# Seven FFNs of 256 tokens computed as seven block products instead of eight

## The chip, the cores and the metric

One core of one Trainium2 chip runs the whole program. The metric is the device time of one execution in microseconds (us); three executions of the kernel before gave 3455.6, 3461.4 and 3465.4 us, median 3461.4.

## The reference, cut to what matters

Two small networks run one after the other on a sequence of 256 tokens of width 1024, all in fp32. Eight feed-forward parts (FFNs) take most of the arithmetic:

```python
def swiglu(y, w_gu, w_down):
    gate, up = jnp.split(y @ w_gu, 2, axis=-1)        # w_gu: 1024 x 5632
    return (jax.nn.silu(gate) * up) @ w_down          # w_down: 2816 x 1024

def half_ffn(h, m, off, g, w_gu, w_down):
    y = modulate(h, g, m[off], m[off + 1])
    return h + 0.5 * m[off + 2] * swiglu(y, w_gu, w_down)
```

The first FFN handles the 256 tokens and 256 context tokens together (512 columns); the other seven handle 256 tokens. Between them lie the mixers (rwkv, conv, gla, mla) and the norms. The modulation vectors `m` are products of a vector with large matrices, `silu(c) @ ada_w`.

## The kernel before, in words

Channels lie on the 128 partitions and tokens along the free axis, so activations are tiles of 128 x 256. `F[0]` is the FFN with 512 columns; `F[1]` to `F[7]` are the seven with 256, and only these are touched. The change reaches all engines.

**One FFN before.** SyncE loads the weights into two buffers `W` in turn (`load_gu`, L2114; `load_down`, L2121); a buffer is freed when the last matmul of the unit two before it has run (`free`, which waits on `s_mm`). A gate unit `u` (11 of them, `PAIRS`) covers 256 gate and the matching 256 up columns: two blocks of 128 (`q`), each with 8 matmuls for gate and 8 for up (L2221). ScalarE takes the Silu of gate (L2302), VectorE multiplies by up (L2427) into `H` in `ARENA`. A down unit (4 of them) gives two blocks of 128 output channels with 22 matmuls each (L2241); VectorE adds them, scaled, onto `X` (L2438). A matmul in fp32 shows in the profile as two records of MATMUL on PE and two of LDWEIGHTS on PEld, so one FFN of 256 columns has 11 x 32 x 2 = 704 records in L2221 and 4 x 44 x 2 = 352 in L2241. The loops over units are real loops of two units.

**Modulation rows.** `ada(g)` on VectorE (L2360 on, with L2370 and L2372) handles a group of four tiles of 128 x 1024: per tile one scalar_tensor_tensor of ADAW with the broadcast vector CB, summed into one column of MOD. GpSimd issues the load of a group (L2180) into one of two buffers and first waits on `s_acc` until the group two before it is through. The lists `groups` say how many groups a unit handles: `F[1]` has `[1,1,0,1,1,0,1,1,0,1,1]` for its gate units and one in each down unit, `F[2]` to `F[4]` have `few = [1,0,1,1,0,1,0,1,1,0,1]` and one in each down unit, `F[5]` to `F[7]` none. On GpSimd these loads are the only work outside the rwkv mixer.

**Between FFNs.** After the last down unit the squares (ScalarE), their sum over channels (PE with `ones`), the root (ScalarE) and `rms` or `layer_norm` (VectorE) make the next input `Y` in four pieces, on which the first matmuls of the next gate unit wait one after the other (`s_y`).

The order of work on every engine is the program's order; nothing is planned at run time.

Of the kernel before, what the change touches and what calls it, by code (L numbers as in the profile page):

```python
# [7 lines left out]
ALU = mybir.AluOpType  # L8
# [145 lines left out]
def build(nc, t, out, table_at, stop=None):  # L154

    stop = STOP if stop is None else stop
    with ExitStack() as ctx:
# [74 lines left out]
        count = {"w": 0, "t": PRE, "silu": 0}  # L232

        def ffn(gu, down, T, groups, mod, k, scale):
# [9 lines left out]
            count["silu"] += FT  # L244
            plan.append(sec)
# [1490 lines left out]
        def mla_phases(layer):  # L1736
# [166 lines left out]
            def dve(dve, V, link):  # L1903
# [84 lines left out]
        F += [ffn(f2[0], d2[0], S, [1, 1, 0, 1, 1, 0, 1, 1, 0, 1, 1] + [1] * 4, 0, 8, 0.5),  # L1988
              ffn(f1[1], d1[1], S, few, 1, 2, 0.5)]
        mixers["conv"] = conv_plan()  # L1990
        F += [ffn(f2[1], d2[1], S, few, 1, 8, 0.5),
              ffn(fi[0, 0], fo[0, 0], S, few, 2, 2, 0.5)]
        mixers["gla"] = gla_plan()
        F += [ffn(fi[0, 1], fo[0, 1], S, [0] * 15, 2, 8, 0.5),
              ffn(fi[1, 0], fo[1, 0], S, [0] * 15, 3, 2, 0.5)]
        mixers["mla"] = mla_plan()
        F += [ffn(fi[1, 1], fo[1, 1], S, [0] * 15, 3, 8, 0.5)]
# [28 lines left out]
        def x_waits(k=DT, n_x=None):  # L2026

            n_x = n["x"] if n_x is None else n_x
            return ([(s_ev, done_t[0] - (DT - k))] if done_t[0] > PRE else [(s_x, 16)]) + ([(s_xr, n_x)] if n_x else [])

        done_t = [PRE]

        def norm(layer, k, T):
            n_rs = sum_squares(T, 1.0 / D, "rms")
            add("rms", layer, 3 * k, T, n_rs, vec("norm_g", 24 * layer + 8 * k, 8), bump("y"))

        def feed(i, layer, k, w):
# [62 lines left out]
        def _(sp):  # L2100
# [65 lines left out]
        def _(pool):  # L2166
            for g, (layer, tile) in enumerate(ADA_GROUPS):
# [430 lines left out]
```

## Time and profile before

| | value |
|---|---|
| executions | 3455.6, 3461.4, 3465.4 us (median 3461.4) |
| profiled execution | 3461.62 us, its span 3459.8 us, mean granted clock 0.954 |
| PE busy | 3168.7 us (92%), 21256 records |
| weight loads busy | 2538.3 us (73%) |
| VectorE / ScalarE / GpSimd busy | 1082.5 / 454.2 / 196.6 us |
| HBM read | 509.44 MB, 148 GB/s over the span |
| largest group | L2221, 5632 matmul records, busy 1383.2 us |

PE is matmul, PEld weight load, DVE VectorE, ACT ScalarE, POOL GpSimd, SPq SyncE's DMA queue. The busy time of PE counts records that overlap in the pipeline only once, so the distance between the starts of two records, not the length of one, is the pace. "Idle before" is the wait of an engine ahead of an instruction, with what ended it. The granted clock has two levels, 1.00 (2.4 GHz) and 0.50 (1.2 GHz).

### The profile page before, as it was taken

Reading aid. Unit: us, or ns where it says so; the run is one execution under the profiler, and the core shown is the slowest. Engines: PE = TensorE matmul, PEld = TensorE weight load, DVE = VectorE, ACT = ScalarE, POOL = GpSimd, SP = SyncE. Lnnn points to the kernel's source line nnn. Section 1 sums busy time; section 2 is a strip of 40 time slices with the busy share of each in tenths; the row PEclk is TensorE's granted clock in tenths of the full one; section 3 lists DMA queues with packets and bytes.
Section 4 is the critical chain, followed back from the end, with each engine's and each line's share of the span. In section 5 each row is a group of like instructions: output and inputs, shape, how many; then the busy total and the mean of one; then the engine's idle time right before and its main releaser. Section 6 shows DMA issues by size and latency. Waiting matters only on the chain.

```text
span 3459.8 us, 48396 instructions
## 1 busy us (share of the span) xinstructions
PE 3168.7 (92%) x21256; PEld 2538.3 (73%) x21256; DVE 1082.5 (31%) x2071; ACT 454.2 (13%) x1034; POOL 196.6 (6%) x314
## 2 busy tenths in 40 slices
PE   7999998777878999999999999989799999979998
PEld 6444445676777888887888878868678878857887
DVE  1554324444355323322632332234320020023101
ACT  1000002333242100001200000023000000021000
POOL 0000001332231000000000000000000000000000
PEclk8999999898899999999999999999699999988999
DMA  5555532002102677575266756534134435412352
GB/s 221 195 174 183 198 147 70 14 4 86 62 4 88 211 250 279 204 267 209 86 202 235 265 208 240 188 102 139 55 119 148 158 105 161 148 64 73 122 164 79
DMA packets 361806, 512.84 MB, mean 148 GB/s; under 512 B 10848, under 2 KB 349856, under 8 KB 352048
## 3 DMA queue, kind: packets, MB, share of 16 engines
q1 hardware_dynamic: 350992, 364.11, 32.6%
q0 software_dynamic: 10080, 143.66, 10.6%
q8 instruction: 125, 2.05, 0.2%
q10 hardware_dynamic: 576, 2.75, 0.2%
q14 instruction: 33, 0.27, 0.0%
HBM read 509.44 MB, written 1.05 MB: 148 GB/s over the span
## 4 chain that ended last, share of the span: by engine, by line
PE 88%; DVE 5%; ACT 2%; issue 2%; DMA 2%; POOL 1%; SPq 0%; DVEq 0%; ACTq 0%; POOLq 0%
PE PS L2221 39%; PE PS L2241 20%; PE PS L488 8%; PE PS L508 4%; PE PS L657 4%; PE PS L2252 2%; PE PS L2200 2%; PE PS L1231 1%; PE PS L1325 1%; PE PS L1450 1%; PE PS L524 1%; PE PS L2274 1%; ACT ADAW L790 1%; DVE X L2532 1%; POOL W L1019 0%
## 5 line engine op out<-in xcount | busy, mean ns | idle before, releaser
L2221 PE MATMUL PS<-Y,W 128*128 128x256 f32 (+1 forms) x5632 | 1383.2, 409 | 41.3 <-DVE Y L2500 26.6
L2221 PEld LDWEIGHTS PS<-Y,W 128*128 128x128 f32 x5632 | 1075.7, 191 | 348.0 <-issue 207.5
L2241 PE MATMUL PS<-ARENA,W 128*128 128x256 f32 (+1 forms) x2816 | 688.4, 407 | 13.5 <-DVE ARENA L2427 7.3
L2241 PEld LDWEIGHTS PS<-ARENA,W 128*128 128x128 f32 x2816 | 536.7, 191 | 165.1 <-issue 90.7
L2427 DVE TENSOR_TENSOR ARENA<-SIL,PS 128x256 f32<-128x256 f32 (+1 forms) x176 | 79.9, 454 | 1011.8 <-ACT SIL L2302 857.7
L2372 DVE SCALAR_TENSOR_TENSOR ADAW<-ADAW,CB 128x1024 f32<-128x1024 f32 x272 | 319.3, 1219 | 6.1 <-DMA ADAW<-in_ada_rows 5.9
L2302 ACT ACTIVATE SIL<-PS 128x256 f32<-128x256 f32 (+1 forms) x176 | 72.3, 411 | 1355.1 <-PE PS L2221 1355.1
L488 PE MATMUL PS<-Y,W 128*128 128x256 f32 (+2 forms) x816 | 183.4, 388 | 32.1 <-DVE Y L2500 22.2
L2438 DVE SCALAR_TENSOR_TENSOR X<-PS,HG,X 128x256 f32<-128x256 f32 x72 | 34.1, 482 | 544.0 <-PE PS L2241 544.0
L488 PEld LDWEIGHTS PS<-Y,W 128*128 128x128 f32 (+2 forms) x816 | 156.4, 192 | 58.9 <-DVE Y L2500 23.0
L508 PE MATMUL PS<-W 64*64 64x64 f32 x4608 | 117.8, 227 | 45.9 <-ACT W L754 24.5
L657 PE MATMUL PS<-Y,W 128*128 128x256 f32 x560 | 134.6, 402 | 24.4 <-DVE Y L2464 15.3
L2314 ACT ACTIVATE Y<-X 128x512 f32<-128x512 f32 x60 | 36.0, 627 | 884.6 <-DVE X L2517 437.7
L657 PEld LDWEIGHTS PS<-Y,W 128*128 128x128 f32 x560 | 111.8, 202 | 47.6 <-DVE Y L2464 16.2
L508 PEld LDWEIGHTS PS<-W 64*64 64x64 f32 x4608 | 104.6, 139 | 57.0 <-issue 27.8
L2180 POOL DMA_DIRECT2D ADAW<-in_ada_rows x68 | 36.1, 531 | 1534.2 <-DVE ADAW L2372 1454.3
L488 PE MATMUL PS<-ARENA,W 128*128 128x256 f32 x480 | 106.9, 383 | 14.4 <-issue 13.8
L488 PEld LDWEIGHTS PS<-ARENA,W 128*128 128x128 f32 x480 | 92.0, 192 | 27.9 <-issue 14.6
L2252 PE MATMUL PS<-Y,CT 128*128 128x256 f32 (+1 forms) x208 | 63.9, 468 | 12.8 <-ACT Y L2314 12.8
L2370 DVE SCALAR_TENSOR_TENSOR JUNK<-ADAW,CB 128x1024 f32<-128x1024 f32 x56 | 68.2, 1217 | 3.0 <-DMA ADAW<-in_ada_rows 3.0
L2200 PE MATMUL PS<-SC,ARENA 128*128 128x2 f32 x256 | 52.3, 343 | 18.1 <-DMA CT<-in_table 18.1
L2252 PEld LDWEIGHTS PS<-Y,CT 128*128 128x128 f32 x208 | 44.8, 218 | 30.2 <-issue 23.9
(346 smaller groups left out, 2160.8 us busy)
## 6 DMA issues: line engine op xcount, KB each, us to landing
ADAW<-in_ada_rows POOLq DMA_DIRECT2D x68, 2048.0 KB, 8.3
W<-in_ffn_w_gu SPq DMA_DIRECT2D x88, 1024.0 KB, 7.5
W<-in_ffn_in SPq DMA_DIRECT2D x88, 1024.0 KB, 6.7
W<-in_ffn_w_down SPq DMA_DIRECT2D x32, 1408.0 KB, 9.0
W<-in_ffn_out SPq DMA_DIRECT2D x32, 1408.0 KB, 8.7
W<-in_even_w_in SPq DMA_DIRECT2D x40, 512.0 KB, 4.6
W<-in_e_w_in SPq DMA_DIRECT2D x34, 512.0 KB, 4.9
ARENA<-in_ada_columns SPq DMA_DIRECT2D x4, 2048.0 KB, 25.3
```

The lines of the kernel that those rows point to most:

```text
L488: last = mm(PS[idx % 4][0:m_, 0:S], wide(c, kt, n_)[:, k, q * P:q * P + m_], x(k), start=(k == 0), stop=(k == kt - 1))
L508: last = mm(to, x, y, start=(k == 0), stop=(k == len(pairs) - 1))
L657: last_ = mm(PS[at[f] % 4][:, 0:S], wide(c, DT, cols)[:, k, q * P:(q + 1) * P], Y[:, k, off:off + S], start=(k == 0), stop=(k == DT - 1))
L2180: pool.dma_start(ADAW[:, g % 2].rearrange("p a b -> p (a b)"), t["ada_rows"][g * P:(g + 1) * P, :])\
L2200: last = mm(PS[c][:, 2 * q:2 * q + 2], PREW[:, c, k, q * P:(q + 1) * P], SC[:, :, k], start=(k == 0), stop=(k == DT - 1))
L2221: last = mm(o, gate_up(c)[:, g, k, q * P:(q + 1) * P], Y[:, k, 0:T], start=(k == 0), stop=(k == DT - 1))
L2241: last = mm(PS[idx % 4][:, 0:T], wide(c, FT)[:, k, q * P:(q + 1) * P], H[:, k, 0:T], start=(k == 0), stop=(k == FT - 1))
L2252: last = mm(NORM_PS[:, 0:T], ones, src[:, k, 0:T], start=(k == 0), stop=(k == kt - 1))
L2302: A(SIL[:, u % 2, 0:T], PS[bank % 4][:, 0:T], ACT.Silu).then_inc(s_silu, 1)
L2370: V.scalar_tensor_tensor(JUNK[:, :], w, 1.0, CB[:, 1], ALU.mult, ALU.mult, accum_out=MOD[:, 4, tile + i:tile + i + 1]).then_inc(s_junk, 1)
L2372: ins = V.scalar_tensor_tensor(w, w, 1.0, CB[:, 1 if layer > 1 else 0], ALU.mult, ALU.mult, accum_out=MOD[:, layer, tile + i:tile + i + 1])
L2427: V.tensor_tensor(H[:, f, 0:T], SIL[:, q, 0:T], up, ALU.mult).then_inc(s_ev, per // 2)
```

## The change: seven block products in place of eight

For `F[1]` to `F[7]` the product of weights and tokens is cut into 2 x 2 blocks, and the blocks of the result are formed from seven block products (Strassen's scheme in Winograd's form) in place of eight. Tokens are cut into two halves of `HT` = 128 columns, and the contraction into two halves. In a gate unit the two weight rows of blocks are gate and up; in a down unit they are the two blocks of 128 output channels.

The names in the new code: `A11`..`A22` are weight blocks and `B11`..`B22` token blocks; the weight sums are S1 = A21 + A22, S2 = S1 - A11, S3 = A11 - A21, S4 = A12 - S2, the token sums T1 = B12 - B11, T2 = B22 - T1, T3 = B22 - B12, T4 = B21 - T2. Product 1 is A11 B11, 2 is A12 B21, 3 is S4 B22, 4 is A22 T4, 5 is S1 T1, 6 is S2 T2, 7 is S3 T3. Each product of a gate unit is two blocks of 128 columns of weights x 4 steps of contraction = 8 matmuls of 128 x 128 weights on 128 tokens (16 records); each product of a down unit has 11 (22 records).

What each engine does now (the diff shows the tables, then GpSimd, PE and VectorE in this order):

- **PE** (`small_ffn`) runs the products in the order 1, 4, 2, 6, 7, 5, 3 (in the first unit 1, 2, 6, 4, 7, 5, 3), each behind its own waits. 2 is accumulated onto 1, and 5 onto 6. The units are unrolled.
- **GpSimd** makes S1 and S3 of each unit once the weights have landed (elements per partition: 1024 in a gate unit, 1408 in a down unit), then the token sums T1 to T4 of the hidden block of the unit before (128 elements each), and last issues the loads of modulation rows, each with its old wait on `s_acc`. S3 is written over A21.
- **VectorE** makes S2 and S4 of each unit at the head of the unit's work, joins the blocks out of PSUM, multiplies, and keeps the groups of modulation rows, now in three parts (two tiles, one, one) between the joins. S2 of an FFN's first unit is made before the norm's reciprocal (`first_sum`).
- **ScalarE** copies product 1 out of PSUM, takes the Silu of one half out of PSUM and of the other out of SBUF.
- **SyncE** loads the same weights as before, under the same rule for free buffers, unrolled.

```diff
+        BX, BY, BQ, BZ, BW = (0, 1), (2, 3), (4, 4), (6, 6), (7, 7)
+        FIRST_ORDER = (1, 2, 6, 4, 7, 5, 3)
+        ORDER = (1, 4, 2, 6, 7, 5, 3)
+        PRODUCT = {1: ("A11", "B11", BX), 2: ("A12", "B21", BX), 3: ("S4", "B22", BW), 4: ("A22", "T4", BQ),
+                   5: ("S1", "T1", BY), 6: ("S2", "T2", BY), 7: ("S3", "T3", BZ)}
...
+            def weight_sums(n_, c, w):
+                pool.wait_ge(s_w[c % 2], 32 * (c // 2 + 1))
+                G.tensor_tensor(w["S1"], w["A21"], w["A22"], ALU.add).then_inc(s_s1, 1)
+                pool.wait_ge(s_s1, n_ + 1)
+                G.tensor_tensor(w["S3"], w["A11"], w["A21"], ALU.subtract).then_inc(s_s3, 1)
...
+            def small_ffn(sec):
+                g = sec["group0"]
+                for u in range(PAIRS + 4):
+                    c, n_ = sec["w0"] + u, sec["n0"] + u
+                    weight_sums(n_, c, gate_blocks(c, n_) if u < PAIRS else down_blocks(c, n_))
+                    if 0 < u < PAIRS:
+                        hidden_sums(sec, u - 1)
+                    for _ in range(sec["groups"][u]):
+                        if g + 2 < len(ADA_GROUPS):
+                            rows(g + 2)
+                        g += 1
...
+                def gate_waits(u, p):
+                    fa, fd = fa0 + 3 * u, fd0 + 5 * u
...
+                    elif p == 3:
+                        pe.wait_ge(s_s4, n0 + u + 1)
...
+                    elif p == 5:
+                        pe.wait_ge(s_fd, fd + 1)
+                    elif p == 6:
+                        pe.wait_ge(s_s2, n0 + u + 1)
...
+                    elif p == 7:
+                        pe.wait_ge(s_s3, n0 + u + 1)
...
+                for u in range(PAIRS):
+                    if u:
+                        second_sum(n_, w)
+                    else:
+                        token_sums(YB, s_ty, 4 * i)
+                    fourth_sum(n_, w)
+                    if more:
+                        ada(g, (0, 1))
+                    dve.wait_ge(s_fa, fa + 1)
+                    dve.wait_ge(s_mm, product_done(sec, u, 6))
+                    V.tensor_tensor(halves(U3), halves(C1), both_banks(BY), ALU.add).then_inc(s_fd, 1)
+                    if more:
+                        ada(g, (2,))
...
+                    V.tensor_tensor(halves(U3), halves(U3), both_banks(BZ), ALU.add).then_inc(s_fd, 1)
...
+                    link(V.tensor_tensor(halves(U3), halves(U3), both_banks(BQ), ALU.add))
+                    V.tensor_tensor(HC[:, u, :, 0:HT], halves(U3), halves(S0), ALU.mult).then_inc(s_fd, 1)
+                    dve.wait_ge(s_mm, product_done(sec, u, 5))
+                    V.tensor_tensor(halves(U4), halves(C1), both_banks(BY), ALU.add).then_inc(s_fd, 1)
...
+                    dve.wait_ge(s_mm, product_done(sec, u, 3))
+                    V.tensor_tensor(halves(C12), halves(U4), both_banks(BW), ALU.add).then_inc(s_fd, 1)
+                    link(V.tensor_tensor(halves(U4), halves(U4), both_banks(BZ), ALU.add))
+                    if more:
+                        ada(g, (3,))
+                        g += 1
+                    dve.wait_ge(s_fa, fa + 3)
+                    V.tensor_tensor(HC[:, u, :, HT:S], halves(U4), halves(C12), ALU.mult).then_inc(s_ev, 7)
+                dve.wait_ge(s_ev, td)
+                token_sums({name: v[:, PAIRS - 1] for name, v in HB.items()}, s_tl, 4 * i)
```

A down unit on VectorE has S2 and S4 (1408 elements), then eight scaled additions onto `X` and three plain ones, of 128 columns each, with the group's tiles between them. Product 4 of the first down unit waits for the token sums of the last hidden block.

## Rows read from the trace of the kernel before

**Rows 1.** The page: busy time, share of the span, instructions.
```profile
PE 3168.7 (92%) x21256; PEld 2538.3 (73%) x21256; DVE 1082.5 (31%) x2071; ACT 454.2 (13%) x1034; POOL 196.6 (6%) x314
```
**Rows 2.** The chain in order of time: start us, us, what.
```profile
1395.29 154.03 PE PS L2221 x704
1550.51 76.24 PE PS L2241 x352
1904.38 16.48 DMA W<-in_ffn_w_down
```
**Rows 3.** Stretches: length, busy (x records) PE, PEld, DVE, ACT, POOL; clock, DMA, GB/s.
```profile
1395.30:1549.30 154.00, 154.00 (x704) 134.53 (x704) 45.02 (x87) 8.07 (x21) 3.69 (x7) 0.99 0.68 235
2557.70:2712.40 154.70, 153.21 (x702) 133.25 (x700) 13.83 (x34) 8.08 (x22) 0.00 (x0) 0.99 0.44 141
```
**Rows 4.** Timeline of PE, matmuls on 128 columns: start us, us, engine, line.
```profile
3146.00 0.83 PE L1825 MATMUL PS<-ADAW 128*128 128x128 f32 x6
3146.67 0.60 PE L1833 MATMUL PS<-ADAW,ARENA 128*128 128x256 f32 x2
3147.10 0.38 PE L1834 MATMUL PS<-ADAW,ARENA 128*128 128x128 f32 x2
3147.32 0.39 PE L1812 MATMUL PS<-ARENA 128*128 128x128 f32 x2
3147.64 0.48 PE L1813 MATMUL PS<-ARENA 64*128 64x128 f32 x2
3148.06 0.49 PE L1814 MATMUL PS<-CT 128*128 128x128 f32 x2
```
**Rows 5.** VectorE by shape: busy us, mean ns of one, idle before.
```profile
L1618 DVE TENSOR_TENSOR ARENA<-ARENA,ADAW 128x1024 f32<-128x1024 f32 x1 | 1.2, 1226 | 0.0
L2427 DVE TENSOR_TENSOR ARENA<-SIL,PS 128x256 f32<-128x256 f32 x154 | 64.8, 421 | 857.7 <-ACT SIL L2302 857.7
L2456 DVE TENSOR_TENSOR Y<-X,RS 128x512 f32<-128x512 f32 x32 | 22.0, 688 | 0.6
```
**Rows 6.** Timeline of GpSimd alone in the rwkv mixer.
```profile
642.31 0.58 POOL L1019 TENSOR_TENSOR W<-ARENA,W 128x192 f32<-128x192 f32 x1
647.77 1.00 POOL L1025 TENSOR_TENSOR W<-W,CT 128x384 f32<-128x384 f32 x1
```
**Rows 7.** Timeline where VectorE and GpSimd both read two SBUF operands.
```profile
956.12 1.02 DVE L947 TENSOR_TENSOR Y<-ARENA 128x512 f32<-128x512 f32 x1
956.55 1.03 POOL L1020 TENSOR_TENSOR W<-ARENA,W 128x192 f32<-128x192 f32 x1
957.17 0.96 DVE L948 TENSOR_TENSOR Y<-Y,ARENA 128x512 f32<-128x512 f32 x1
```
**Rows 8.** Timeline from the last gate unit to the first down unit.
```profile
1310.84 0.42 DVE L2427 TENSOR_TENSOR ARENA<-SIL,PS 128x256 f32<-128x256 f32 x1 [6.49 <-ACT SIL L2302]
1311.17 1.22 DVE L2372 SCALAR_TENSOR_TENSOR ADAW<-ADAW,CB 128x1024 f32<-128x1024 f32 x1
1311.58 1.59 PEld L2241 LDWEIGHTS PS<-ARENA,W 128*128 128x128 f32 x8 [1.60 <-DVE ARENA L2427]
1312.32 1.22 DVE L2372 SCALAR_TENSOR_TENSOR ADAW<-ADAW,CB 128x1024 f32<-128x1024 f32 x1
```
**Rows 9.** Timeline of VectorE: two pieces of the norm's output.
```profile
1395.06 0.68 DVE L2456 TENSOR_TENSOR Y<-X,RS 128x512 f32<-128x512 f32 x1
1396.43 0.68 DVE L2456 TENSOR_TENSOR Y<-X,RS 128x512 f32<-128x512 f32 x1
```
**Rows 10.** Stretches, columns as in rows 3: a gap and what follows.
```profile
1310.40:1312.40 2.00, 0.81 (x4) 0.74 (x5) 1.56 (x4) 0.38 (x1) 0.00 (x0) 1.00 0.65 211
1917.80:1921.20 3.40, 0.22 (x1) 0.23 (x2) 3.00 (x6) 0.37 (x1) 0.00 (x0) 1.00 0.80 270
1921.80:1925.00 3.20, 3.20 (x9) 2.57 (x8) 1.40 (x4) 0.00 (x0) 0.53 (x1) 0.50 1.09 359
```
**Rows 11.** Loads of W, 1156 to 2200 us: time to landing.
```profile
DMA to landing us min/median/max: 3.4/6.4/16.5
```

More of the change, by code:

```diff
@@ L244, in ffn, with small_ffn @@
             count["silu"] += FT
+            plan.append(sec)
+            return sec
+        def small_ffn(gu, down, groups, mod, k, scale):
+            n_ = PAIRS + 4
+            sec = dict(kind="small", gu=gu.rearrange("(k p) n -> p k n", p=P), down=down.rearrange("(k p) n -> p k n", p=P),
+                       T=S, groups=groups, w0=count["w"], t0=count["t"], n0=count["sums"], i=count["sums"] // n_, mod=mod,
+                       k=k, scale=scale)
+            sec["fa0"] = sec["i"] * (3 * PAIRS + 4)
+            sec["fd0"] = sec["i"] * (5 * PAIRS + 6 * 4)
+            sec["td"] = sec["t0"] + 7 * PAIRS
+            sec["ends"] = [sec["t0"] + 7 * (j + 1) for j in range(n_)]
+            sec["t1"] = sec["ends"][-1]
+            count["w"] += n_
+            count["t"] = sec["t1"]
+            count["sums"] += n_
             plan.append(sec)
@@ L278, in build @@
+        s_s1, s_s2, s_s3, s_s4 = [sem(f"weight_sum{i}_ready") for i in range(1, 5)]
+        s_ty = sem("token_sums_ready")
+        s_th = sem("hidden_sums_ready")
+        s_tl = sem("last_hidden_sums_ready")
+        s_fa = sem("small_ffn_scalar_step")
+        s_fd = sem("small_ffn_vector_step")
         HP = 2 * HD
@@ L2140, in _ @@
                         load_down(sec, j, j)
+                elif sec["kind"] == "small":
+                    for j in range(PAIRS):
+                        free(sec["w0"] + j)
+                        load_gu(sec, j, j)
+                    for j in range(4):
+                        free(sec["w0"] + PAIRS + j)
+                        load_down(sec, j, j)
                 else:
@@ L2358, in _, with ada @@
             link = Chain(dve, s_dve)
[L2360 removed]
+            def ada(g, part=range(GROUP)):
                 layer, tile = ADA_GROUPS[g]
[L2363 to L2364 removed]
+                if part[0] == 0:
+                    dve.wait_ge(s_adaw[g % 2], 16 * (g // 2 + 1))
+                for i in part:
                     w = ADAW[:, g % 2, i]
@@ L2550, in _ @@
                     ffn(F[args[0]])
+                elif kind == "small":
+                    small_ffn(F[args[0]])
+                elif kind == "first_sum":
+                    first_sum(args[0])
                 elif kind == "do":
```

301 lines of the change are left out of this document (260 added, 41 removed).

## The prediction

> **What bounds the kernel now.** I read the busy times first: PE's matmuls fill 92% of the span, VectorE 31%, ScalarE 13%, GpSimd 6% [rows 1]. The chain of waits in order of time then shows an FFN of 256 tokens as two unbroken pieces of PE: 704 records in 154.03 us and 352 in 76.24 us [rows 2]. In the stretches PE is busy without a gap at a clock of 0.99, while in an FFN with modulation rows VectorE works 45.0 of 154.0 us and the DMA share is 0.68; in one without them VectorE works 13.8 us and the share is 0.44 [rows 3]. So PE's pace is the bound: 76.24 / 352 = 0.2166 us for a record of 256 columns. An FFN has 1056 such records, 228.7 us. Its small gaps are one of 1.6 us between gate and down, where PE waits for the last multiplication [rows 8], and one at the start: the input comes in pieces 1.37 us apart [rows 9], of which a piece feeds 4 records, 0.87 us, so three waits cost 1.5 us.
>
> **Fewer, but shorter matmuls.** A product of a gate unit has 16 records, seven of them 112, 11 units 1232; a product of a down unit has 22, so 7 x 22 x 4 = 616. Together 1848 records of 128 columns in place of 1056 of 256. The arithmetic falls by an eighth, but each block of weights is used for half as many columns, so the loads per unit of time nearly double. What matters is the distance between two records on 128 columns with 128 x 128 weights. In the mla mixer six run in a row and the next begins 0.67 us after the first: 0.1117 us each; two more (L1834) take 0.22 us, 0.110 each [rows 4]. I take 0.1117: 206.4 us, against 228.7. Gain 22.3 us an FFN; at 0.110 it would be 25.4. In a gate unit a product then lasts 1.79 us and the unit 12.5 us (before 13.9); in a down unit 2.46 and 17.2 us (before 19.1).
>
> On the weight loads a page speaks against this. In L1825's six records every matmul loads new weights over all 128 rows and still follows the last after 0.1117 us [rows 4], so the load runs beneath the matmul before it. The Trainium skill ("TensorE: Matmul & The Clock Gate", What overlaps and what doesn't) says that a weight load overlaps matmuls in flight only where the row group differs. By that rule load and matmul would take turns, 0.223 us a record, 413 us an FFN and some 4750 us in all; the trace does not agree.
>
> **Where each unit's sums come from.** GpSimd alone takes 0.58 us for 192 elements and 1.00 for 384 [rows 6], so 2.2 ns an element: 2.4 us for 1024, 3.2 for 1408, 0.44 for 128. VectorE takes 1.226 us for 1024 and 0.421 for 256 [rows 5]: 1.63 for 1408 and 0.29 for 128. A tile of modulation rows takes 1.22 us, and the next starts after 1.15 [rows 8], so two take 2.37. Where both engines read two SBUF operands at once, 512 elements on VectorE take 1.02 and 0.96 us [rows 7] in place of 0.688 [rows 5], and 192 on GpSimd 1.03 [rows 7] in place of 0.58 [rows 6]: factors 1.45 and 1.75.
>
> VectorE's work in a gate unit without rows is 2.45 us of sums and eight joins of 0.42, 5.8 us; with a group of rows 10.5 us. GpSimd's is 2 x 2.4 + 4 x 0.44 = 6.6 us. Both fit in 12.5 us, so the order decides, not the load.
>
> *Unit without rows behind a unit without rows.* Weights land 6.4 us (3.4 to 16.5) after their issue [rows 11], which is a whole unit ahead, so S1 and S3 exist before the unit starts or soon after. VectorE finishes the last unit 1.6 us into the new one (add 0.2 to 0.6, add, Silu, multiply) and has S2 by 3.3 and S4 by 5.0, contention counted. Product 6 starts at 5.4, product 3 at 10.7. The first join after product 6 (done 7.2) ends at 7.8, product 5 starts at 9.0. No stall; a unit with rows behind it has two tiles more (7.4) and its join ends by 7.9. Still none. ScalarE's copy of product 1 takes 0.38 us (8.07 us for 21 records of 256 columns [rows 3]) and lies under product 4.
>
> *Any unit behind a unit with rows.* GpSimd's load of the next group stands ahead of the next unit's S1, and waits until VectorE has ended the fourth tile, which now comes after product 3. With zero at the end of product 3: VectorE adds twice (to 1.07) and ends the tile at 2.35; GpSimd issues the load, 0.53 us (3.69 us for 7) [rows 3], to 3.0; S1 to 5.4; S2 under contention 1.8 us to 7.3; PE restarts 0.3 us after a release, as between multiply and down unit [rows 8]: product 6 at 7.6 in place of 5.4. S3, slowed, comes at some 9.5 and costs 0.2 more. Stall 2.4 us. If this unit has rows too, S4 ends at 9.1, two tiles under contention (3.4) at 12.5, the join at 12.9, and product 5 starts at 13.2 in place of 11.4: 1.8 more, 4.2 in all. The bounds: with no contention 1.6 and 2.0; with VectorE shut out for the whole of each GpSimd operation 4.0 and 6.3 (S2 waits for S3 and ends at 9.1).
>
> Counting the lists: `F[1]` has three units of the first and four of the second kind: 3 x 2.4 + 4 x 4.2 = 24.0 us. `F[2]` to `F[4]` have four and two: 18.0 us each. `F[5]` to `F[7]`: none.
>
> *Gate to down.* Without rows: multiply done at 1.6, three chained sums of 0.29 with links to 2.6, product 4 at 2.9 in place of 2.5: 0.4 us, against 1.6 before, a gain of 1.2. With rows: product 4 at 4.5 (2.0 late), and the join ahead of product 5 is 0.6 late: 2.6, a loss of 1.0. In the other down units the group's last tile lies ahead of the joins of product 5, so GpSimd is released 2.5 us before the unit ends, and product 6 is due 7.4 us in: no stall. The late landing in `F[3]`, 16.48 us [rows 2], stays a late landing, since it has 12.5 us in place of 13.9; its wait falls on that of product 4. Under 1 us, left out.
>
> *First unit.* Product 1 ends at 2.7, product 2 waits for ScalarE's copy (3.4) and piece four (4.1) and ends at 5.4, product 6 needs two sums of 512 elements after the last piece: 6.0. Two products are 3.6 us, so 2.4 is lost, against 1.5 before: 0.9. S2 of the first unit is made while VectorE waits for the norm's root; nothing is late by it.
>
> **The sum.** `F[5]` to `F[7]`: 22.3 - 0.9 + 1.2 = 22.6 us, three times 67.8. `F[2]` to `F[4]`: 22.3 - 0.9 - 18.0 - 1.0 = 2.4, three times 7.2. `F[1]`: 22.3 - 0.9 - 24.0 - 1.0 = -3.6. Together 71.4 us off the profiled execution's 3461.62 us (span 3459.8, with 1.8 around it): 3390 us. The median of the runs, 3461.4, is the same within 0.2.
>
> **The rivals.**
>
> *The weight load is exposed at every product.* Each of the 11 x 7 + 4 x 7 = 105 products of an FFN begins behind waits and with new blocks. Between L1812, L1813 and L1814 a pair takes 0.42 us (3147.64 to 3148.06) in place of 0.22 [rows 4]: the load was not ahead. For it: seven times as many waits as before. Against it: L1825 to L1833 and L1834 to L1812 cross a wait at 0.11 us [rows 4]; the slow pairs are those where the weights change from 128 rows to 64 and back. Price 105 x 0.20 = 21 us an FFN, 147 in all: 3537 us. It decides from 5.5 ns a record (71.4 us over 7 x 1848), that is from a mean pace of 0.117 us. Slower than before.
>
> *VectorE is shut out while GpSimd works.* Rows 7 show slowing, not shutting out, but over 0.6 us operations. Gate stalls then are 28.6 in place of 18.0 us and 37.2 in place of 24.0: 45 us more, 3435 us. The same end is reached if stalls make the clock fall: a gap of 1.6 us left it at 1.00, one of 3.4 us was followed by 0.50 for 3.2 us [rows 10], 1.6 us lost each time, and there are 25 stalls of 2.4 to 4.2 us (25 x 1.6 = 40). The Trainium skill ("SBUF — State Buffer", Who interferes with whom) has a VectorE operation with two SBUF inputs contend with GpSimd's reads, and in its Terms the loser fully blocks; that gives this rival's number, and rows 7, where both advance, agree only in part.
>
> *The stalls are small and the pace is the fast one.* With no contention 34 us less stall, with 0.110 us a record 22 us more gain: 3334 us.
>
> *No change,* by partial forms of these: for it speaks only that four of the seven FFNs gain almost nothing.
>
> **Chances.** Forecast 0.55; small stalls 0.17; shutting out or clock 0.15; exposed loads 0.10; no change 0.03. Range 3330 to 3440 us: it reaches to the second and third case and leaves out the exposed loads, no change, and the ends of these. The forecast's own range is 3360 to 3420. A change under 0.3%, 10 us, can't be told from none. Faster: 0.55 + 0.17 + 0.15 = 0.87; within: 0.03; slower: 0.10.
>
> **What would show it.** Over an FFN without rows (`F[5]`), PE should go through 1232 records in about 140 us and 616 in 69, with starts 0.11 us apart also across products. In `F[2]` the unit behind one with rows should have PE waiting 2 us for VectorE's S2 ahead of product 6, VectorE waiting for GpSimd's S1, and GpSimd for the fourth tile; the gate part of `F[1]` should last some 162 us (1232 x 0.1117 + 24.0 + 0.9). A pace above 0.117, stalls in `F[5]`, or GpSimd's 1024 elements at 3.5 us instead of 2.4 would prove me wrong.

## The result, and the profile after

The kernel with seven block products takes 3462.93 us (median of 20 runs, 3455.68 to 3467.94), the kernel before 3456.97 us (20 runs, 3449.29 to 3465.40). The ratio is 1.0017, with a 95% interval of 1.0010 to 1.0024: slower, but by less than the 0.3% named above as no change. The forecast was 3390 us, a gain of 2.1%, with a range of 3330 to 3440. The forecast was wrong, and the time fell outside the range.

The profiled execution of the new kernel has a span of 3458.8 us at a mean clock of 0.944; before it was 3459.8 us at 0.954. First its busy times (columns as in [rows 1]):

```profile
PE 3056.9 (88%) x26800; PEld 2609.0 (75%) x26800; DVE 1901.0 (55%) x3023; ACT 493.4 (14%) x1139; POOL 1052.8 (30%) x804
```

PE has less to do than before (3056.9 in place of 3168.7 us) and the span is the same: PE now stands still for 401.9 us in place of 291.1. VectorE and GpSimd have 1675 us more between them, in which their waiting for each other is counted (below). The stretches of `F[2]` (gate, down) and of `F[5]` (gate, down), columns as in [rows 3]:

```profile
1410.00:1574.00 164.00, 146.78 (x1226) 142.23 (x1227) 122.64 (x174) 13.91 (x33) 100.69 (x66) 0.97 0.60 213
1574.00:1653.00 79.00, 71.76 (x622) 71.60 (x621) 70.33 (x88) 3.20 (x8) 28.22 (x13) 0.96 0.63 220
2611.00:2753.00 142.00, 140.43 (x1231) 139.52 (x1232) 78.44 (x126) 13.90 (x33) 80.21 (x59) 0.98 0.48 155
2753.00:2827.00 74.00, 70.96 (x621) 70.80 (x620) 37.99 (x54) 1.52 (x5) 28.53 (x10) 0.98 0.46 146
```

The gate part of `F[5]` is what was forecast (about 140 us; 142). The down part has 74 us in place of the 69 forecast. `F[2]` has modulation rows: its gate part took 154 us before, now 164, and its down part 79 in place of 76. Where PE waits in the block products stands in the list of PE's waits (after the colon: total us, times, longest):

```profile
PE PS L2473 <- DVE ARENA L2716: 38.1, 7, 7.2
PE PS L2431 <- DVE ARENA L2700: 36.1, 32, 1.3
PE PS L2431 <- DVE SIL L2738: 30.3, 25, 2.2
...
PE PS L2431 <- POOL W L2281: 3.9, 25, 0.2
```

The second line is S2 ahead of product 6 (32 times, of which 25 behind a unit with rows). The third is the join after product 6, for which product 5 waits. The first, the dearest of all, is the last token sum between gate and down part: 5.4 us on average, seven times.

**The seven FFNs, one by one.** From the starts of all PE records I take each FFN apart: the distance between neighbours is 0.112 us (before 0.216), what a distance above 0.36 us (before: above 0.86) has over that is a gap, and what the others have over it is put down to PE at the lower clock. In us:

```
                               F[1]   F[2]   F[3]   F[4]   F[5]   F[6]   F[7]    sum
before: first to last matmul  231.3  231.3  235.2  234.6  233.2  233.3  233.3  1632.2
  at the pace of 0.216        228.1  in each                                  1596.7
  gaps                          1.4    1.4    3.4    3.2    2.5    2.6    3.4    17.9
  lower clock                   1.8    1.8    3.7    3.3    2.6    2.6    1.8    17.6
after: first to last matmul   250.5  243.1  242.5  243.5  215.8  217.3  215.9  1628.6
  at the pace of 0.112        207.0  in each                                  1449.0
  gaps in gate units           26.4   21.5   20.6   22.0    2.5    2.5    2.9    98.4
  gap ahead of product 4        7.4    7.4    7.4    7.4    3.2    3.2    3.2    39.2
  lower clock                   9.7    7.3    7.5    7.1    3.2    4.6    2.8    42.2
PE idle ahead of the FFN, before 4.0    4.0    4.0    8.0    4.8    4.8    4.8    34.4
PE idle ahead of the FFN, after  8.3    4.1    7.2    8.1    6.1    5.8    4.8    44.4
```

So the change gains 147.7 us of pace and gives 144 back inside the FFNs (119.7 in gaps, 24.6 by the clock) and 10 ahead of them: 6.4 us slower. The medians differ by nearly the same, 6.0. The two profiled spans don't show it: the profiled execution of before was 4.7 us above its median, the other 2.3 us below.

### The profile page after: what moved, and what is told of

Read it like the earlier page. It is cut to its first block and busy times, and to the rows that moved or that the text cites. A ratio compares the mean times of both kernels' runs of the same rounds, so it can differ in the third digit from the quotient of the medians.

```text
span 3458.8 us, 60893 instructions
## 1 busy us (share of the span) xinstructions
PE 3056.9 (88%) x26800; PEld 2609.0 (75%) x26800; DVE 1901.0 (55%) x3023; ACT 493.4 (14%) x1139; POOL 1052.8 (30%) x804
## 3 DMA queue, kind: packets, MB, share of 16 engines
q8 instruction: 207, 3.39, 0.4%
## 5 line engine op out<-in xcount | busy, mean ns | idle before, releaser
L2431 PE MATMUL PS<-Y,W 128*128 128x128 f32 x4928 | 599.1, 280 | 55.0 <-DVE Y L2866 27.5
L2431 PEld LDWEIGHTS PS<-Y,W 128*128 128x128 f32 x4928 | 578.0, 196 | 67.4 <-issue 47.0
L2279 POOL TENSOR_TENSOR ARENA<-W 128x1024 f32<-128x1024 f32 (+1 forms) x105 | 270.8, 2579 | 929.8 <-DMA W<-in_ffn_in 595.9
L2431 PE MATMUL PS<-Y,ARENA 128*128 128x128 f32 x3696 | 452.5, 280 | 66.8 <-DVE ARENA L2700 36.1
L2431 PEld LDWEIGHTS PS<-Y,ARENA 128*128 128x128 f32 x3696 | 433.5, 195 | 78.0 <-DVE ARENA L2700 42.2
L2473 PE MATMUL PS<-ARENA,W 128*128 128x128 f32 x2464 | 300.2, 283 | 38.1 <-DVE ARENA L2716 38.1
L2473 PEld LDWEIGHTS PS<-ARENA,W 128*128 128x128 f32 x2464 | 294.4, 200 | 39.2 <-issue 39.2
L2361 PE MATMUL PS<-Y,W 128*128 128x512 f32 x704 | 305.2, 597 | 2.2 <-DVE Y L2830 2.2
L2281 POOL TENSOR_TENSOR W<-W 128x1024 f32<-128x1024 f32 (+1 forms) x105 | 299.3, 2851 | 8.2
L2361 PEld LDWEIGHTS PS<-Y,W 128*128 128x128 f32 x704 | 134.8, 192 | 172.0 <-issue 171.4
L2700 DVE TENSOR_TENSOR ARENA<-ARENA,W 128x1024 f32<-128x1024 f32 (+1 forms) x105 | 167.2, 1592 | 81.3 <-POOL ARENA L2279 81.0
L2705 DVE TENSOR_TENSOR ARENA<-W,ARENA 128x1024 f32<-128x1024 f32 x77 | 151.2, 1963 | 2.4
L744 PEld LDWEIGHTS PS<-Y,W 128*128 128x128 f32 x560 | 109.7, 198 | 46.1 <-DVE Y L2830 16.2
## 6 DMA issues: line engine op xcount, KB each, us to landing
ADAW<-in_ada_rows POOLq DMA_DIRECT2D x68, 2048.0 KB, 10.4
```

The source lines that it names most:

```text
L744: last_ = mm(PS[at[f] % 4][:, 0:S], wide(c, DT, cols)[:, k, q * P:(q + 1) * P], Y[:, k, off:off + S], start=(k == 0), stop=(k == DT - 1))
L2279: G.tensor_tensor(w["S1"], w["A21"], w["A22"], ALU.add).then_inc(s_s1, 1)
L2281: G.tensor_tensor(w["S3"], w["A11"], w["A21"], ALU.subtract).then_inc(s_s3, 1)
L2361: last = mm(o, gate_up(c)[:, g, k, q * P:(q + 1) * P], Y[:, k, 0:T], start=(k == 0), stop=(k == DT - 1))
L2431: last = mm(block_bank(b, q), w[left][:, k, q * P:(q + 1) * P], YB[right][:, k], start=(k == 0 and p not in (2, 5)), stop=(k == 3), skip_g ...
L2473: last = mm(block_bank(b, 0), w[left][:, k], HB[right][:, k], start=(k == 0 and p not in (2, 5)), stop=(k == PAIRS - 1), skip_group_check= ...
```

## Why the gaps: one engine works, the other stands

The timeline behind a unit with rows in `F[2]`; product 3 of that unit ended at 1425.9, and products 1, 4 and 2 of the next last until 1431.3:

```profile
1428.05 0.42 DVE L2759 TENSOR_TENSOR ARENA<-SIL 128x256 f32<-128x256 f32 x1
1428.42 0.58 POOL L2273 DMA_DIRECT2D ADAW<-in_ada_rows  x1 [24.82 <-DVE ADAW L2628]
1429.02 2.36 POOL L2279 TENSOR_TENSOR ARENA<-W 128x1024 f32<-128x1024 f32 x1
...
1431.42 1.23 DVE L2700 TENSOR_TENSOR ARENA<-ARENA,W 128x1024 f32<-128x1024 f32 x1 [2.95 <-POOL ARENA L2279]
1431.46 3.39 POOL L2281 TENSOR_TENSOR W<-W 128x1024 f32<-128x1024 f32 x1
1432.68 3.26 DVE L2705 TENSOR_TENSOR ARENA<-W,ARENA 128x1024 f32<-128x1024 f32 x1
...
1432.70 2.05 PE L2431 MATMUL PS<-Y,ARENA 128*128 128x128 f32 x16 [1.34 <-DVE ARENA L2700]
1434.81 1.44 POOL L2288 TENSOR_TENSOR ARENA<-ARENA 128x128 f32<-128x128 f32 x1
...
1435.86 0.41 DVE L2738 TENSOR_TENSOR SIL<-JUNK,PS 128x256 f32<-128x256 f32 x1
1436.33 0.46 POOL L2290 TENSOR_TENSOR ARENA<-ARENA 128x128 f32<-128x128 f32 x1
```

The chain forecast is there step by step: the load issued behind VectorE's tile, 2.5 us after product 3, then S1 (L2279), S2 (L2700), product 6 at 6.8. But nothing is slowed by a factor. S2 needs 1.23 us, its time alone. S3 (L2281) is issued 0.04 us after it and takes 3.39: it waits 1.03 us for S2 and then takes its own 2.36. S4 (L2705) is issued 1.22 us after S3 and takes 3.26: it waits until S3 has ended, some 2.1 us, and then takes its own 1.2. GpSimd's token sum (L2288) in turn waits 1.0 for S4 and then takes its 0.46. The join L2738 reads one operand from PSUM; it takes its 0.41 whatever GpSimd does. The Trainium skill ("SBUF — State Buffer", Who interferes with whom, and Terms) says just this: a VectorE instruction with two SBUF inputs contends with a GpSimd one that reads SBUF, whoever is first holds the ports for its whole instruction, and the other fully blocks. The trace agrees to 0.1 or 0.2 us: S3 ends 2.20 us after S2, S4 1.09 us after S3 and the token sum 0.31 us after S4, each that much under its time alone.

What that does to a short operation stands between gate and down part, where product 4 waits for three chained token sums of 0.29 us:

```profile
1574.68 2.62 PE L2473 MATMUL PS<-ARENA,W 128*128 128x128 f32 x22
...
1577.34 0.29 DVE L2712 TENSOR_TENSOR ARENA<-ARENA 128x128 f32<-128x128 f32 x1
1577.67 3.52 DVE L2714 TENSOR_TENSOR ARENA<-ARENA 128x128 f32<-128x128 f32 x1
1577.86 3.16 POOL L2279 TENSOR_TENSOR ARENA<-W 128x1408 f32<-128x1408 f32 x1
1581.10 3.15 POOL L2281 TENSOR_TENSOR W<-W 128x1408 f32<-128x1408 f32 x1
1581.22 3.18 DVE L2716 TENSOR_TENSOR ARENA<-ARENA 128x128 f32<-128x128 f32 x1
...
1584.54 0.77 PE L2473 MATMUL PS<-ARENA,W 128*128 128x128 f32 x2 [7.24 <-DVE ARENA L2716]
```

S1 and S3 of the down unit run unhindered (3.16, 3.15), and the two sums on which PE waits are late by a whole one each: 3.52 and 3.18 us for 0.29 us of work. Even L2714, issued 0.19 us ahead of S1, lost. Without rows GpSimd is already through S1, and only S3 is in the way: 3.2 us.

The groups by shape (busy us, mean ns of one, idle before) show how wide this reaches. S4, and the additions onto `X`, of which the form that reads PSUM has 351 ns and the form that reads SBUF twice 1542:

```profile
L2705 DVE TENSOR_TENSOR ARENA<-W,ARENA 128x1024 f32<-128x1024 f32 x77 | 151.2, 1963 | 2.4
L2775 DVE SCALAR_TENSOR_TENSOR X<-SIL,HG,X 128x128 f32<-128x128 f32 x84 | 129.5, 1542 | 2.0
...
L2775 DVE SCALAR_TENSOR_TENSOR X<-PS,HG,X 128x128 f32<-128x128 f32 x112 | 39.3, 351 | 59.6 <-PE PS L2473 55.4 <-issue 0.5
```

**The clock.** Stretches around that gap, columns as in [rows 3]:

```profile
1581.90:1584.50 2.60, 0.00 (x0) 0.00 (x0) 2.60 (x2) 0.00 (x0) 2.35 (x1) 0.62 0.98 404
1584.60:1588.00 3.40, 3.40 (x16) 3.40 (x17) 3.37 (x3) 0.00 (x0) 0.00 (x0) 0.50 0.94 368
1588.00:1591.40 3.40, 3.40 (x27) 3.40 (x27) 2.08 (x4) 0.00 (x0) 0.00 (x0) 0.80 0.47 149
1591.40:1650.00 58.60, 58.60 (x528) 58.60 (x527) 53.34 (x68) 2.50 (x6) 20.76 (x9) 1.00 0.59 207
```

After 7.2 us without work PE runs 16 records in 3.4 us at 0.50, that is at 1.2 GHz, in place of some 30 at 2.4. A mean of 0.80 over the next 3.4 us is 1.4 us more at 0.50 and 2.0 at 1.00. The last row has the pace undisturbed: 58.60 / 528 = 0.111 us.

The small stalls look different. The first row below holds two stalls of `F[2]`'s gate part, of 1.5 and 2.3 us, and the clock stays at 1.00; the second is the one stretch at 0.50 in the middle of that part; the third is the start of the FFN:

```profile
1459.20:1468.20 9.00, 5.34 (x43) 4.77 (x42) 7.95 (x8) 0.38 (x1) 8.77 (x6) 1.00 0.91 352
1541.60:1544.80 3.20, 3.20 (x15) 3.20 (x16) 2.15 (x5) 0.00 (x0) 1.27 (x1) 0.50 0.00 0
1410.20:1415.00 4.80, 4.24 (x17) 3.65 (x18) 4.62 (x11) 0.59 (x2) 0.00 (x0) 0.50 0.25 79
```

In all seven gate parts together the clock is at 0.50 for 59 us, before for 24. Of these 42 lie at the starts of the FFNs (before all 24), and 17 in five single stretches of 3.4 us, two in `F[1]` and one each in `F[2]` to `F[4]`.

**Ahead of the norm.** S2 of an FFN's first unit stands before the norm's reciprocal:

```profile
1142.93 2.35 POOL L2281 TENSOR_TENSOR W<-W 128x1024 f32<-128x1024 f32 x1
1142.95 3.40 DVE L2700 TENSOR_TENSOR ARENA<-ARENA,W 128x1024 f32<-128x1024 f32 x1 [4.36 <-POOL ARENA L2279]
...
1146.47 1.75 DVE L2837 RECIPROCAL RS<-RS 128x256 f32<-128x256 f32 x1
```

ScalarE's root was ready at 1142.0. VectorE waited for S1 till 1142.9, S2 lost to S3 and took 3.40, and the norm, for which PE stands still, began 4.3 us late. Ahead of `F[3]` it is the same (3.2 us). Ahead of `F[5]` and `F[6]` S2 is through in time; there a piece of the norm (L2896) takes 1.97 and 1.72 us in place of 0.68, beside GpSimd's S3 of the second unit.

## The experiments

Each ratio is against the kernel before, run on the same chip, with its 95% interval; the median of before was 3457.38 us in the first four, 3451.12 in the next three, and 3452.71 in the last two. The changed kernel itself stands at 1.0017. "Gaps" are taken as in the table above.

**1. The loads of rows wait a unit.** GpSimd issues a group's load behind the next unit's S1 and S3, so these no longer wait for VectorE's fourth tile.

```diff
                     weight_sums(...)
+                    while due:
+                        rows(due.pop(0))
...
                     for _ in range(sec["groups"][u]):
                         if g + 2 < len(ADA_GROUPS):
-                            rows(g + 2)
+                            due.append(g + 2)
```

> The changed kernel, with GpSimd issuing the loads of modulation rows one unit later, behind the next unit's S1 and S3. Theory A (order and lock): the time is lost because GpSimd's load stands ahead of the next unit's S1, and because VectorE and GpSimd shut each other out when both read two SBUF operands. Then the gate gaps of the FFNs with rows, 21 to 26 us in the changed kernel, should fall to some 8 to 14 us each, the low clock should shrink with them, and the time should be 35 to 60 us below the changed kernel's, about 3410 us. Theory B (weights late): units of 12.5 us instead of 13.8 outrun the weight loads. Then nothing moves by more than 5 us.

Measured: 3404.15 us (3398.61 to 3413.73), ratio 0.9851 (0.9826 to 0.9877). The gate gaps of `F[1]` to `F[4]` fell from 90.5 to 42.9 us: that link of the chain was real. But PE's idle time ahead of `F[1]`, `F[3]` and `F[4]` rose to 11.1, 11.0 and 12.1 us. With no load in the way, the second unit's S1 and S3 now run beside the norm, and its pieces take 1.63 and 2.63 us where they took 0.69 and 0.73:

```profile
1153.21 1.63 DVE L2826 TENSOR_TENSOR Y<-X,RS 128x512 f32<-128x512 f32 x1
1154.38 2.67 POOL L2281 TENSOR_TENSOR W<-W 128x1024 f32<-128x1024 f32 x1
1154.88 2.63 DVE L2834 TENSOR_SCALAR Y<-Y,GS,MOD 128x256 f32<-128x256 f32 x2
```

The same contention, in another place, and of another kind of operation: L2834 reads one tensor from SBUF, with two factors of one element per partition. The first of its two took 2.31 us, in place of 0.41, and ended just after S3.

**2. The first down unit's weight sums behind the last token sums.**

```diff
                     c, n_ = sec["w0"] + u, sec["n0"] + u
+                    if u == PAIRS:
+                        pool.wait_ge(s_tl, 4 * sec["i"] + 4)
                     weight_sums(...)
```

> The changed kernel, with GpSimd starting the weight sums of the first down unit only after the token sums of the last hidden block. Theory A: the gap of 7.5 us ahead of product 4 in the first down unit (3.3 us in FFNs without rows) is VectorE's four small sums taking turns with GpSimd's 1408 element sums. It should shrink to 2 to 3 us (under 1 us without rows): 4 x 4.5 + 3 x 2.6 = 26 us, with clock some 30 us below the changed kernel, about 3432 us. Theory B: the gap is the weights' landing or the last multiply; it stays above 6 us and the time moves by less than 5 us.

Measured: 3428.95 us (3424.78 to 3440.66), ratio 0.9924 (0.9896 to 0.9951), 0.93% or 32 us less than the changed kernel. PE's waits for the last token sum and, new, for the join after product 6 of that unit:

```profile
PE PS L2475 <- DVE SIL L2788: 6.0, 4, 1.5
PE PS L2475 <- DVE ARENA L2718: 5.1, 7, 1.1
```

From 38.1 us to 5.1, by one wait. The down part's gaps fell by 22.9 us, and its time at the lower clock by 12.2 (from 13.4 to 1.2), while the gate part kept both. So the clock's loss there hung on this gap: each of the four gaps of 7.4 us cost some 2.0 us more than its length, each of the three of 3.2 us some 1.4.

**3. GpSimd's sums on one column.** All of GpSimd's sums shrink to one element per partition; S1, S3 and the token sums of the hidden blocks are thus left out. Everything waits for the same semaphores.

```diff
+                one = slice(0, 1)
-                G.tensor_tensor(w["S1"], w["A21"], w["A22"], ALU.add)...
+                G.tensor_tensor(w["S1"][:, 0, one], w["A21"][:, 0, one], w["A22"][:, 0, one], ALU.add)...
```

> The changed kernel with every GpSimd sum of the block products cut to one column of 128 partitions (the rest of the sums is left out), all waits and the order kept. Theory A: with no long GpSimd operation there is nothing to wait for and nobody to shut out. The FFNs should take 211 to 216 us each, gate gaps under 5 us, gap ahead of product 4 of the first down unit under 1.5 us, and the time should be about 3320 us (3305 to 3345). Theory B: gaps stay, time above 3420 us. If the low clock came from the short matmuls and not from the gaps, the FFNs would keep 10 us or more at the low clock with the gaps gone.

Measured: 3345.73 us (3340.06 to 3347.57), ratio 0.9675 (0.9655 to 0.9694): with GpSimd's work gone the change is worth 3.2%. Its S2 and S4 are back at their time alone, and the largest wait in the gate units is now a load:

```profile
L2706 DVE TENSOR_TENSOR ARENA<-W,ARENA 128x1024 f32<-128x1024 f32 x77 | 94.4, 1226 | 2.4
L2701 DVE TENSOR_TENSOR ARENA<-ARENA,W 128x1024 f32<-128x1024 f32 x77 | 94.1, 1222 | 25.2 <-POOL ARENA L2280 24.8
```

```profile
PE PS L2432 <- DMA W<-in_ffn_w_gu: 16.9, 12, 2.1
```

The idle time ahead of `F[1]` and `F[3]` is 4.0 again. I expected some 3320, and gate gaps under 5 us in each FFN; in `F[1]` to `F[4]` they are 7.4 to 10.4. The weights themselves come late, up to 2.1 us, which the stalls had covered. The low clock did not go with the gaps either: in the seven FFNs together it is at 0.50 for 64 us (103 in the changed kernel, 31 before), most of it at their starts. This run takes away both GpSimd's hold on the ports and its latency, so it doesn't tell these two apart.

**4. Block products in `F[5]` to `F[7]` alone.** `F[1]` to `F[4]` as before.

```diff
-        F += [small_ffn(f2[0], d2[0], ...), small_ffn(f1[1], d1[1], few, 1, 2, 0.5)]
+        F += [ffn(f2[0], d2[0], S, ...), ffn(f1[1], d1[1], S, few, 1, 2, 0.5)]
```

> Block products only in the last three FFNs, which have no modulation rows; the first four of 256 tokens as in the kernel before. Theory A: each of the three is 16 to 17.5 us shorter than before, less some 2 us in all for the first S2 ahead of the norms: 46 to 51 us below the kernel before, about 3409 us. A theory in which the seven FFNs are coupled (weights, queues) would give less than 35 us.

Measured: 3406.01 us (3402.66 to 3415.89), ratio 0.9861 (0.9837 to 0.9885). The three took 217.0, 215.8 and 217.8 us, against 233.3 before: the gain of 48 us is theirs, and the four with rows had cost more than that.

**5. Both orders together.** Edits 1 and 2, and in the first unit S3 behind S2 in place of behind S1.

```diff
-                pool.wait_ge(s_s1, n_ + 1)
+                pool.wait_ge(s_s2 if behind else s_s1, n_ + 1)
                 G.tensor_tensor(w["S3"], ...)
```

> The changed kernel with both earlier edits (loads of modulation rows one unit later; first down unit's sums behind the last token sums), and in an FFN's first unit GpSimd makes S3 only after VectorE's S2. Theory A (order and lock): the gains add up, save that the boundary gap of the FFNs with rows was already partly gone: 15 to 30 us below the kernel with late rows alone (3404 us), so about 3382 us (3372 to 3392); the idle time ahead of F[1] falls from 11.1 to 6 or 7 us. Theory C (VectorE's amount of work in the units with rows, not its turns with GpSimd, sets the gaps): under 10 us.

Measured: 3401.93 us (3397.59 to 3405.48), ratio 0.9854 (0.9837 to 0.9870), no better than edit 1 alone, where 3372 to 3392 was expected. The down gaps of `F[1]` to `F[4]` were 8.2 to 11.1 us, at a new place, ahead of product 5 of the first down unit:

```profile
1562.88 4.17 DVE L2634 SCALAR_TENSOR_TENSOR ADAW<-ADAW,CB 128x1024 f32<-128x1024 f32 x1
1566.98 0.08 DVE L2634 DVE_READ_ACCUMULATOR ADAW<-ADAW,CB 128x1 f32 x1
1566.98 4.15 DVE L2634 SCALAR_TENSOR_TENSOR ADAW<-ADAW,CB 128x1024 f32<-128x1024 f32 x1
```

With its load no longer waiting for VectorE, GpSimd goes from one unit's S1 and S3 to the next's with only 0.57 us between (four sums, 1553.64 to 1570.06). VectorE's S4 takes 4.46 us, the two tiles behind it 4.17 and 4.15 in place of 1.22, and the join behind those is 7.4 us late. The old place of the load had kept GpSimd out of VectorE's way here. The number alone would fit the rival, that VectorE's amount of work sets the gaps; the next two runs speak against it.

**6. The fourth tile early.** Edit 2, S3 behind S2 in the first unit, the loads where the change has them, and the fourth tile of a group beside the third, ahead of the joins after products 7, 5 and 3. In `F[2]` the fourth tile then ends 1.5 us before product 3 does, in place of 2.2 us after it.

```diff
                     if more:
-                        ada(g, (2,))
+                        ada(g, (2, 3))
+                        g += 1
...
-                    if more:
-                        ada(g, (3,))
-                        g += 1
```

> The changed kernel with the fourth tile of each group of modulation rows handled beside the third, ahead of products 7, 5 and 3, in place of the load issued later; with the edits for the first down unit and the first unit's S3. Theory A: GpSimd is released some 2 us before the unit ends in place of 2.4 us after, so S1 of the next unit is there in time, and the multiply is no longer behind a tile: gate gaps of F[1] to F[4] from 21 to 26 us down to 6 to 12, total about 3365 us (3345 to 3385), lower than with late rows. Theory C: the work of VectorE is the same, only moved, so above 3400 us.

Measured: 3361.59 us (3356.98 to 3366.78), ratio 0.9741 (0.9725 to 0.9757). Gate gaps in `F[1]` to `F[4]` 49.4 us (from 90.5), down gaps 1.2 to 2.5. VectorE's busy time, waiting counted, is 1902.3 us, as in the changed kernel (1901.0), and the kernel is 2.8% faster: what fell is not what VectorE does or waits in all, but what PE waits for it.

**7. All sums on VectorE.** GpSimd only issues loads; VectorE makes S1 to S4 at the head of a unit and T1 to T4 behind its last multiplication. The order is otherwise that of the change.

```diff
+                V.tensor_tensor(w["S1"], w["A21"], w["A22"], ALU.add).then_inc(s_s1, 1)
                 V.tensor_tensor(w["S2"], w["S1"], w["A11"], ALU.subtract).then_inc(s_s2, 1)
+                V.tensor_tensor(w["S3"], w["A11"], w["A21"], ALU.subtract).then_inc(s_s3, 1)
```

> The changed kernel with all sums on VectorE: S1 and S3 beside S2 and S4, and the token sums after each multiply; GpSimd only issues loads. VectorE's work grows by 3.7 us a gate unit, to 9.5 us without rows and 14.2 with, in a unit of 12.5 us. Theory A: no VectorE operation takes longer than it does alone. F[5] to F[7] should take 212 to 214 us (gap ahead of product 4 under 1 us), the units with rows should be bound by VectorE at some 14.5 us, 2 to 3 us of gap each, F[1] to F[4] 224 to 230 us; total 3370 to 3400 us, clearly below the changed kernel's 3462. Theory C: more work on the engine that sets the gaps makes it slower than the changed kernel, above 3465 us.

Measured: 3359.88 us (3359.51 to 3364.63), ratio 0.9736 (0.9719 to 0.9752), better than expected. Busy times:

```profile
PE 3033.9 (90%) x26800; PEld 2592.2 (77%) x26800; DVE 1954.6 (58%) x3513; ACT 492.9 (15%) x1139; POOL 196.4 (6%) x314
```

This run shows what the helper saved VectorE. VectorE executes 490 instructions more than in the changed kernel, 210 weight sums (154 of 1.22 us, 56 of 1.62) and 280 token sums of 0.29, 359 us in all, and its busy time grows by only 54. The other 305 us had thus been in its records as waiting for GpSimd, which spent 856 us to spare VectorE 54. No weight sum takes longer than alone (1217 to 1224 ns for 1024 elements). How much of the 2.8% gained is the ports' and how much GpSimd's latency the run doesn't say: S1 is also made in 1.22 us in place of 2.36, and no longer stands behind a load that waits for the fourth tile.

**8. Token sums on VectorE, weight sums on GpSimd.** Edit 6, with T1 to T4 of the hidden blocks moved to VectorE.

> As the version with the fourth tile beside the third, but the sums of a hidden pair (four of 128 columns) are made by VectorE right behind the multiplication that ends the pair, not by GpSimd. If the two engines take turns on the SBUF operands, what counts is the time that both need together: a string of four takes GpSimd some 4 to 6 us with its handovers and VectorE 4 x 0.29 = 1.2 us undisturbed. Theory (turns): the stalls ahead of product 6 and 5 in units with modulation rows shrink, 3350 to 3356 us in place of 3361.6. Rival (what stands first on VectorE decides): S2 and S4 of each unit with rows start 1.2 us later on VectorE, which is on the path, 23 units x up to 1.2 = 3375 us or more.

Measured: 3377.92 us (3373.21 to 3380.74), ratio 0.9775 (0.9760 to 0.9789): slower than edit 6. The rival was right in kind. The string stands ahead of S2, and what comes before it is late besides:

```profile
1453.11 1.13 DVE L2745 TENSOR_TENSOR ARENA<-SIL 128x256 f32<-128x256 f32 x1 [0.25 <-ACT SIL L2544]
1454.27 0.29 DVE L2700 TENSOR_TENSOR ARENA<-ARENA 128x128 f32<-128x128 f32 x1
...
1455.34 1.22 DVE L2688 TENSOR_TENSOR ARENA<-ARENA,W 128x1024 f32<-128x1024 f32 x1
```

S2 (L2688) now makes PE wait 33.7 us, 37 times, where in edit 6 it was 6.3 us, 17 times. Less work for both engines together isn't enough; the order on the path counts too.

**9. All sums on VectorE, and the fourth tile early.** Edit 7 with the tile order of edit 6.

> All sums on VectorE as in the run before, and the fourth tile of a group beside the third, ahead of the joins of products 7, 5 and 3. Theory (the order decides): VectorE no longer comes late out of a unit with rows, so the gate gaps of 17.6, 14.3, 14.7 and 13.0 us fall below 10 and the time to some 3345 us. Rival (the load decides): in a gate unit with rows VectorE alone has 4 x 1.22 us of tiles, 4 x 1.22 of sums, 4 x 0.29 of token sums and 8 x 0.42 of joins, 14.3 us against the unit's 12.5, so moving a tile moves the wait to the joins of 7 and 5 and the time stays at 3360 us within 5.

Measured: 3340.78 us (3338.98 to 3343.77), ratio 0.9674 (0.9661 to 0.9688), the best of all and 3.3% below the kernel before. Against edit 6, with the same order of tiles, that is 0.7% for taking the sums off GpSimd. The gate gaps of `F[1]` to `F[4]` are 11.8, 8.5, 9.0 and 8.5 us (17.6, 14.3, 14.7 and 13.0 in edit 7); below 10 was expected for all four. The rival, that VectorE's load decides, falls: in `F[2]`'s gate part it works 129.8 of 149.0 us and PE has 142.7 (columns as in [rows 3]):

```profile
1382.00:1531.00 149.00, 142.74 (x1233) 140.36 (x1233) 129.79 (x236) 13.89 (x33) 3.69 (x7) 0.99 0.69 235
1531.00:1600.20 69.20, 69.03 (x619) 68.86 (x617) 57.35 (x95) 3.08 (x8) 2.11 (x4) 1.00 0.76 263
```

The down part runs without a gap. The FFNs take 221.4, 218.2, 218.6, 218.9, 213.5, 213.7 and 213.8 us, 114 us less than before, of the 148 that the pace gives.

## Why the prediction was wrong

**The pace was right.** 0.112 us a record against 0.1117 forecast; the 21.1 us gained in each FFN are the 22.3 less 1.2, half of it from the old pace (0.2160, not 0.2166). The rival of the exposed weight load falls: records follow at 0.11 us across products too.

**GpSimd's own times were right**: 2.36 us for 1024 elements (forecast 2.4), 3.16 for 1408 (3.2), 0.46 for 128 (0.44).

**The gate stalls came out right in sum, with a wrong mechanism in part.** Forecast were 94.8 us, the 2.4 of each first unit included; measured 98.4. `F[1]` has 7 distances of 1.61 between starts and 4 of 2.43, as many as the list of rows gives (3 + 4, and 4). Over the pace these are gaps of 1.5 and 2.3 us; S3 adds one of 0.3 each time (0.2 forecast). But the forecast had 2.4 and 1.8 for stalls of 1.8 and 2.3: it took S2 as slowed to 1.8 us, and it ran in 1.23; the loss came one step later, in S4, and was larger. Not foreseen were small gaps (0.66 and 0.96 between starts) in units with rows behind units without, where GpSimd's token sums take turns with S4 and the tiles. The two errors cancel. One good sum is no proof of its terms. The 162 us named for `F[1]`'s whole gate part had 0.9 for the first unit where the working has 2.4, so 164 was meant; it took 171.7, 7.3 of them by the clock.

**The step from gate to down, 2.6 us with rows and 0.4 without, failed; measured 7.4 and 3.2.** This is the largest missed term, 27.6 us. The working counted the token sums as "three chained sums of 0.29 with links" and did not ask what GpSimd does at that moment. It had contention as a factor on an operation's own length (1.45 and 1.75, from [rows 7]); but what is paid is the rest of the other's operation, and for 0.29 us of work behind a 3.16 us operation that is a factor of 12. [Rows 7] themselves allow the right reading: 0.96 less 0.688 is a wait of 0.27 us, 1.03 less 0.58 one of 0.45, each shorter than the other engine's operation. From operations of similar, small size slowing and waiting look alike. The rival of the shut-out VectorE had the rule right, but priced it in the gate units alone, and there too high (28.6 us in `F[2]` without the first unit, measured 21.5 with it, since S2 won its turn against S3), and got 0.15.

**The clock, for which the sum has no term, failed: 24.6 us.** Of this 12.2 us hang on the gap between gate and down part, as edit 2 shows. The rest lies in the gate parts, where the time at 0.50 grew by 35 us, about half of it at the FFNs' starts and half in the five stretches named above; no run isolates what brings it. The stalls of 1.5 and 2.3 us that come every 12 us or so mostly left the clock at 1.00. [Rows 10] had the price, 1.6 us after a gap of 3.4; the forecast named it in a rival and left it out of the sum.

**"Nothing is late by it" (S2 ahead of the norm) failed.** Of the 10.0 us of added idle time ahead of the FFNs 7.5 lie ahead of `F[1]` and `F[3]`, where VectorE waits for GpSimd, which waits for a load, and the norm stands behind. Another 2.3 lie ahead of `F[5]` and `F[6]`, where not S2 but GpSimd's S3 of the second unit holds up the norm's pieces.

**The old gaps were taken at 1.5 + 1.6 us in each FFN**, 21.7 us; they were 17.9. Another 3.8 us less to gain.

Together: 8.4 (pace) + 3.6 (gate) + 27.6 (gate to down) + 3.8 (old gaps) + 24.6 (clock) = 68.0 us, so in place of -71.4 inside the FFNs it was -3.4 (measured -3.6), and +10.0 ahead of them. The chances were wrong with the time: no change had 0.03, as something that only partial forms of the rivals would give. That is what happened; several small terms, each priced at nothing, pointed the same way.

What stays open: what holds the clock at 0.50 for longer at the FFNs' starts (42 us in place of 24, and 47 in edit 9, whose stalls are few), how the time splits between waiting for the ports and GpSimd's latency, and the 8 to 12 us of gate gaps left in edit 9, in part late weights (7.6 us of waits for loads over the whole kernel).

## What to carry to other kernels

Before work is put on GpSimd beside VectorE, list every VectorE operation with two SBUF operands that can fall beside it: each can be late by a whole GpSimd operation, however short it is itself. Put the TENSOR_SCALAR with one SBUF operand on the list too (edit 1). Then look at the order: with all sums still on GpSimd, the order alone turned +0.2% into -2.6% (edit 6). A helper of half the speed may cost its master nearly as much time as the work would; here moving all sums back to VectorE as well gave -3.3%. When a wait is taken away, ask what the freed engine will now run beside.

## What the runs showed of the hardware

- Two operations on VectorE and GpSimd that both read two SBUF operands take turns whole: S3 with 3.39 us in place of 2.36, token sums with 3.52 and 3.18 us for 0.29 us of work; with an operand from PSUM VectorE isn't held (351 against 1542 ns).
- A TENSOR_SCALAR that reads one SBUF tensor of 256 elements took 2.31 us beside S3 in place of 0.41 (edit 1), while in the changed kernel a RECIPROCAL, also with one SBUF operand, kept its 1.75 us though begun (2605.59) in the midst of an S1 (2604.03 to 2606.37).
- A VectorE operation issued 0.19 us ahead of GpSimd's still lost the turn (L2714 at 1577.67, S1 at 1577.86), while S2, 0.04 us ahead of S3, won it (1431.42, 1431.46). By what the Trainium skill says ("SBUF — State Buffer", Who interferes with whom) L2714, as the first to start, would have had the turn; no run here says why it lost.
- GpSimd took 2.36 us for 1024 elements, VectorE 1.22.
- After 7.2 us without matmuls PE ran at 1.2 GHz for another 4.8 us (3.4 + 1.4); matmuls on 128 columns with new 128 x 128 weights each follow at 0.111 us without a break (528 in 58.60 us).
